# Weighted sums over index heads: one product of 128 stationary columns per sequence, or four products of 32 stationary columns for two sequences

## The chip, the cores and the metric

The kernel runs on one core of a Trainium2 chip. The metric is the device time of one execution in microseconds (us). One program computes both layers; there is one launch.

## The reference

One inference step of a two-layer hybrid decoder trunk for a prompt of 1024 tokens and 8 sample sequences of 8 new tokens each, with 8192 cached positions per sample sequence. Three parallel head groups (mLSTM, indexer-selected sparse attention, RWKV-7) read one combined input projection. The part that the change touches is the indexer of the sample sequences:

```
def index_scores(iq, iw, ik, mask):
    s = jnp.einsum('bthd,bsd->bths', iq.astype(jnp.float32), ik.astype(jnp.float32))
    s = jax.nn.relu(s * IDX_DIM ** -0.5)
    score = jnp.einsum('bths,bth->bts', s, iw.astype(jnp.float32) * IDX_HEADS ** -0.5)
    return jnp.where(mask[None], score, -jnp.inf)
```

For every sequence b, new token t and cached position s the dot products of 8 index heads h with the cached index key are taken, cut at zero, and summed over the heads with the token's weights. The 256 highest scores of a token then select the cached rows that are attended to. All arithmetic is float32.

## The kernel before, in words

The front stage (stage_front, line 149) runs once per layer, before all other stages, and stages are separated by barriers of all engines. On TensorE it walks through 72 units (UNITS, line 171), one for each pair of a 512-column slice of the input projection and a tile of 128 tokens: `unit(u)` makes 8 products of 128x128 by 128x512 (line 396), the evictions from PSUM are ScalarE's (line 518), and the first 36 units are rotated by VectorE, transposed by TensorE (line 422) and copied out (line 611).

The indexer's work is spread between these products. A piece J is one sequence's block of 1024 cached keys. There are 64 such pieces, PIECES = 8 blocks for each of DB = 8 sequences, the sequence running fastest (m = J // 8 is the block, b = J % 8 the sequence), and 8 pieces more for the new keys (J from 64 on). Units 10 to 27 take RATE = 4 pieces each, and each piece stands behind a quarter of the unit's projection. For a piece:

- GpSimd gathers two halves of the keys into one of RING = 6 buffers by two indirect DMAs (line 378), six pieces ahead, each as soon as the transposes of the piece that held the buffer are done (semaphore kt_p).
- `turn` (line 431) transposes them, 8 transposes of 128x128 onto 64 columns, into pt[0] and pt[1]; VectorE copies one half (line 640), ScalarE the other (line 534) into kt[J % 2]. The transposes of one piece wait for both copies of the piece before.
- `score` (line 440) is one product of the keys with the queries laid out as a block diagonal, into pi[J % 2], 512 columns: row f*64 + h*8 + t for half f, head h and token t. It waits for the relu of the piece two before.
- `relu` on ScalarE (line 525) goes from pi[J % 2] to rl[J % 2], and waits until the weighted sum of piece J-2 is done.
- `weigh` (line 452) multiplies rl by a stationary 128x128 slice of the table pk ("pick"), which holds the head weights of sequence b in the columns f*64 + b*8 + t and zeros elsewhere. The 8 sequences of a block accumulate in one bank, acc, so that row f*64 + b*8 + t of acc is the score of that token for half f. The piece's work on TensorE is issued as score(J), turn(J+2), weigh(J-1).
- `place` on VectorE (line 646) copies acc into the table of scores s after every 8 pieces; the next block's first weigh waits for it.

For the new keys the products are smaller: score is 64x64 (line 442), weigh 64x128 by 64 columns (line 454).

From unit 29 on VectorE finds the 256th highest score in 32 rounds of counting over the whole table (line 658). TensorE adds up each count after the projection of a unit (line 478). After the last projection two small products (lines 491 and 492) close the ranking, VectorE writes the last tables (lines 707 to 710), and the stage's last DMAs store them.

Every float32 product appears in the trace as two pairs of a stationary load (PEld) and a pass over the moving columns (PE); a transpose appears as one pair.

Of the kernel before, what the change touches and what calls it, by code (L numbers as in the profile page):

```python
# [12 lines left out]
ACT = mybir.ActivationFunctionType  # L13
# [3 lines left out]
P = 128  # L17
# [4 lines left out]
DB = 8  # L22
DT = 8
NS = DB * DT
# [3 lines left out]
HD = 64  # L28
# [120 lines left out]
def stage_front(nc, l, io, sc, const):  # L149
# [23 lines left out]
    NJ = TURNED + DB  # L173
# [3 lines left out]
    BITS = 31  # L177
    N = HALF + NS

    def pieces(u):  # L180
        return range(RATE * (u - START), RATE * (u - START + 1)) if START <= u < ENDED else ()

    with Stage(nc) as st:
# [25 lines left out]
        iwc = st.sb("iw_cols", [P, 2, DB])  # L209
        pk = st.sb("pick", [P, DB * (P + DT)])  # L210
        kt = [st.sb(f"ikT{b}", [P, 4, P]) for b in range(2)]
        rl = [st.sb(f"relu{b}", [P, 512]) for b in range(2)]

        bit = st.sb("bit", [P, BITS], I32)
        bit_f = st.sb("bit_value", [P, BITS])
# [12 lines left out]
        acc = st.ps("p_score", [P, 512])  # L228
        pt = [st.ps(f"pt{i}", [P, 4, P]) for i in range(2)]
        pi = [st.ps(f"pi{i}", [P, 512]) for i in range(2)]  # L230
# [16 lines left out]
        with nc.Block() as block:  # L247
# [119 lines left out]
            @block.gpsimd  # L367
            def _(pool):
                pool.memset(iq[:, :, :, :, :], 0.0).then_inc(zeroed, 1)  # L369
                pool.memset(pk[:, :], 0.0).then_inc(zeroed, 1)  # L370
                pool.wait_ge(idx_r, 1)
                for J in range(TURNED):
                    m, b = J // DB, J % DB
                    if J >= RING:

                        pool.wait_ge(kt_p, J - RING + 1)
                    for f in range(2):
                        pool.indirect_dma_start(ring[J % RING][:, f, :, :].rearrange("p o d -> p (o d)"), None, table,  # L378
                                                bass.IndirectOffsetOnAxis(ap=idx[:, m, 2 * b + f:2 * b + f + 1], axis=0)).then_inc(got[J % RING], 16)

            @block.tensor
            def _(pe):
                def turn_in(o):
                    pe.wait_ge(normed, o + 1)
                    if o:
                        pe.wait_ge(nT_ready, 2 * o)
                    for k in range(KT):
                        ins = pe.transpose(pt[k // 4][:, k % 4, :], xn[o % 2][:, k * P:(k + 1) * P], ident[:, :])
                        if k % 4 == 3:
                            ins.then_inc(xT_psum, 1)  # L390

                def slice_of(u, k0, k1):
                    c, t = UNITS[u]
                    w, cw = (ws, SMALL) if c == IK else (wb[(c - 1) % 2], 512)
                    for k in range(k0, k1):
                        ins = pe.matmul(pp[u % 2][:, 0:cw], nT[:, k, t * P:(t + 1) * P], w[:, k, 0:cw], start=(k == 0), stop=(k == KT - 1))  # L396
                    if k1 == KT:
                        ins.then_inc(chunk_done, 1)

                def unit(u):  # L400
                    c, t = UNITS[u]
                    if c == IK:
                        pe.wait_ge(ws_loaded, 32)
                        pe.wait_ge(nT_ready, 2 * ORDER.index(t) + 2)
                    else:

                        pe.wait_ge(w_loaded[(c - 1) % 2], 16 * ((c - 1) // 2 + 1))
                    if u >= 2:
                        pe.wait_ge(chunk_out, u - 1)
                    n = len(pieces(u)) or 1  # L410
                    for i in range(n):
                        slice_of(u, KT * i // n, KT * (i + 1) // n)
                        if pieces(u):
                            piece(pieces(u)[i])

                def turn_out(u):
                    c, _ = UNITS[u]
                    pe.wait_ge(rotated, u + 1)
                    pe.wait_ge(turned_out, u)
                    v = qo[u % 2] if c in (IK, Q) else pr[u % PR]  # L420
                    for j in range(TURNS[c]):
                        ins = pe.transpose(ptx[:, j, :], v[:, j * P:(j + 1) * P], ident[:, :])
                    ins.then_inc(turned, 1)

                def turn(J):
                    pe.wait_ge(got[J % RING], 32 * (J // RING + 1))
                    if J:
                        pe.wait_ge(kt_r, 2 * J)
                    for f in range(2):
                        for o in range(RUN):  # L430
                            ins = pe.transpose(pt[f][0:HD, o, :], ring[J % RING][:, f, o, :], ident[:, :])  # L431
                    ins.then_inc(kt_p, 1)

                def score(J):
                    b = J % DB
                    if J >= 2:
                        pe.wait_ge(i_r, J - 1)
                    if J < TURNED:
                        pe.wait_ge(kt_r, 2 * J + 2)
                        ins = pe.matmul(pi[J % 2][:, :], iq[:, b, :, :, :].rearrange("p a h t -> p (a h t)"), kt[J % 2][:, :, :], start=True, stop=True)  # L440
                    else:
                        ins = pe.matmul(pi[J % 2][0:HD, 0:NS], iq[0:HD, b, 0, :, :].rearrange("p h t -> p (h t)"), ikn[:, :], start=True, stop=True)
                    ins.then_inc(i_p, 1)

                def weigh(J):
                    m, b = J // DB, J % DB
                    pe.wait_ge(i_r, J + 1)
                    if b == 0 and m:
                        pe.wait_ge(placed, m)
                    w = pk[:, b * P:(b + 1) * P]  # L450
                    if m < PIECES:
                        ins = pe.matmul(acc[:, :], w, rl[J % 2][:, :], start=(b == 0), stop=(b == DB - 1))
                    else:
                        ins = pe.matmul(acc[:, 0:NS], w[0:HD, :], rl[J % 2][0:HD, 0:NS], start=(b == 0), stop=(b == DB - 1))
                    ins.then_inc(w_p, 1)

                def piece(J):
                    score(J)
                    if J + 2 < TURNED:
                        turn(J + 2)  # L460
                    if J:
                        weigh(J - 1)

                def step(u):
                    if 2 <= u < TILES:
                        turn_in(u)
                    if u == START:
                        pe.wait_ge(nT_ready, 2 * TILES)
                        turn(0)
                        turn(1)  # L470
                        pe.wait_ge(iq_r, 1)
                    unit(u)
                    if u == ENDED:
                        weigh(NJ - 1)
                    k = u - COUNT0 - 1
                    if 0 <= k <= BITS:
                        pe.wait_ge(counted, k + 1)
                        pe.matmul(ptot[:, k:k + 1], pair, cnt[:, k:k + 1], start=True, stop=True).then_inc(total, 1)
                    elif k == BITS + 2:
                        pe.wait_ge(fin_c, 1)  # L480
                        pe.matmul(pfin[:, 0:2], pair, fin[:, :], start=True, stop=True)
                        pe.matmul(pfin[:, 2:3], below, fin[:, 1:2], start=True, stop=True).then_inc(fin_p, 1)
                    if 2 <= u < NTURN + 2:
                        turn_out(u - 2)

                turn_in(0)
                turn_in(1)
                for u in range(NU):
                    step(u)
                pe.wait_ge(ranked, 1)  # L490
                pe.matmul(pfin[:, 3:4], below, s[:, HALF - 1:HALF], start=True, stop=True)
                pe.matmul(pfin[:, 4:5], pair, s[:, HALF - 1:HALF], start=True, stop=True).then_inc(rank_p, 1)

            @block.scalar
            def _(act):
# [23 lines left out]

                def relu(J):  # L520
                    act.wait_ge(i_p, J + 1)
                    if J >= 2:
                        act.wait_ge(w_p, J - 1)
                    if J < TURNED:
                        ins = act.activation(rl[J % 2][:, :], pi[J % 2][:, :], ACT.Relu, scale=HD ** -0.5)
                    else:
                        ins = act.activation(rl[J % 2][0:HD, 0:NS], pi[J % 2][0:HD, 0:NS], ACT.Relu, scale=HD ** -0.5)
                    ins.then_inc(i_r, 1)

                def copy_kt(J):  # L530
# [5 lines left out]
                def piece(J):  # L536
                    relu(J)
                    if J + 2 < TURNED:
                        copy_kt(J + 2)
# [3010 lines left out]
```

## Time and profile before

| | |
|---|---|
| median of 3 runs | 6780.59 us |
| the three runs | 6777.11, 6780.59, 6792.77 us |
| the profiled execution, span from its first to its last instruction | 6785.8 us |
| mean granted TensorE clock | 0.868 |
| front stage, layer 0 (from the start to the last tables at 718.0 us) | about a tenth of the span |
| TensorE busy | 5678.2 us, 84% of the span |
| VectorE, ScalarE, GpSimd busy | 2916.9, 1480.2, 741.8 us |

The profile gives no time for the profiled execution besides its span. In the profile, PE is TensorE's passes and PEld its stationary loads (they overlap the passes), DVE is VectorE, ACT is ScalarE, POOL is GpSimd, SP is SyncE. L452 is line 452 of the kernel. The form 128*32 would be a stationary operand of 128 rows and 32 columns, and 128x512 a moving operand of 128 rows and 512 columns. The granted clock is a share of 2.4 GHz. The end of a pass is modelled, so that the durations of neighbouring passes overlap; the distance between starts tells how long TensorE was taken up. The second layer's front stage repeats the first's.

### The profile page before, as it was taken

The page shows a single profiled execution, that of the slowest core. Times are in us where ns is not written, and L with a number is a line of the kernel's source. Part 1 is how long each engine was busy: PE and PEld are TensorE (multiplying, and loading weights), DVE is VectorE, ACT ScalarE, POOL GpSimd, SP SyncE. Part 2 cuts the span into 40 slices and gives each one's busy share as a digit, 9 for nine tenths or more (in the row PEclk, how much of TensorE's full clock was granted, in tenths as well). Part 3 has the DMA queues.
Part 4 walks back from the last instruction along what each step waited for, and adds up shares of the span by engine and source line. Part 5 has one row for each costly group of instructions (what it writes and reads, how often), then busy time and mean ns, then how long its engine had stood idle before and what let it go on. Part 6 is the DMA issues. An engine that isn't in the chain of part 4 may idle for free. (4 is left out here: it accounts for less than half of the span.)

```text
span 6785.8 us, 62816 instructions
## 1 busy us (share of the span) xinstructions
PE 5678.2 (84%) x22554; PEld 3493.1 (51%) x22554; DVE 2916.9 (43%) x6698; ACT 1480.2 (22%) x2844; POOL 741.8 (11%) x776
## 2 busy tenths in 40 slices
PE   6999686465789899999989996863757879999997
PEld 4544464344567456654455444642545664666543
DVE  2257564367644233330032566533775442334200
ACT  2210122046243111100033102221553331110000
POOL 2400175000000000000033003740000000000000
PEclk9999688575789999999989996975757889999998
DMA  4222233120000231121132313322000013211122
GB/s 148 87 93 81 72 109 95 27 67 15 11 19 5 111 131 50 57 69 59 50 117 82 107 68 89 110 71 68 26 14 19 11 61 120 76 57 50 58 74 93
DMA packets 358055, 462.83 MB, mean 68 GB/s; under 512 B 70258, under 2 KB 261172, under 8 KB 357332
## 3 DMA queue, kind: packets, MB, share of 16 engines
q1 hardware_dynamic: 320932, 358.82, 16.4%
q0 software_dynamic: 36864, 100.71, 4.8%
q8 instruction: 144, 2.36, 0.1%
q14 instruction: 115, 0.94, 0.0%
HBM read 347.87 MB, written 121.69 MB: 69 GB/s over the span
## 5 line engine op out<-in xcount | busy, mean ns | idle before, releaser
L396 PE MATMUL pp<-w_in,nT 128*128 128x512 f32 x2016 | 909.3, 597 | 0.0
L3309 PE MATMUL pm<-w_down,hT 128*128 128x512 f32 x1584 | 685.5, 596 | 24.3 <-DMA hT<-scratch_hT 24.3
L3236 PE MATMUL pg<-nT,wgu 128*128 128x364 f32 (+1 forms) x2112 | 670.1, 471 | 16.5 <-DMA wgu<-in_w_up 16.5
L3236 PE MATMUL pu<-nT,wgu 128*128 128x364 f32 (+1 forms) x2112 | 665.1, 468 | 0.0
L396 PEld LDWEIGHTS pp<-w_in,nT 128*128 128x128 f32 x2016 | 375.6, 191 | 428.0 <-issue 427.3
L3236 PEld LDWEIGHTS pg<-nT,wgu 128*128 128x128 f32 x2112 | 403.7, 191 | 261.1 <-issue 21.1
L3236 PEld LDWEIGHTS pu<-nT,wgu 128*128 128x128 f32 x2112 | 401.4, 190 | 242.2
L3309 PEld LDWEIGHTS pm<-w_down,hT 128*128 128x128 f32 x1584 | 302.9, 191 | 406.4 <-issue 406.4
L2478 POOL DMA_INDIRECT k_sel<-in_cache_k,kv_idx x256 | 247.4, 966 | 985.2 <-DVE kv_idx L2622 860.1
L3261 DVE TENSOR_SCALAR sig<-exp_neg 128x364 f32<-128x364 f32 x132 | 46.1, 349 | 680.6 <-ACT exp_neg L3247 680.6
L3262 DVE RECIPROCAL exp_neg<-sig 128x364 f32<-128x364 f32 x132 | 319.4, 2419 | 4.5
L3327 DVE TENSOR_TENSOR x_tile<-pm,x_tile 128x512 f32<-128x512 f32 x36 | 24.9, 691 | 685.1 <-PE pm L3309 685.1
L378 POOL DMA_INDIRECT ik<-in_cache_idx_k,idx x256 | 245.0, 957 | 390.2 <-PE pt L431 338.2
L658 DVE TENSOR_SCALAR_CACHE_REDUCE area<-s,cand 128x4160 f32<-128x4160 f32 x62 | 281.8, 4546 | 2.2
L3247 ACT ACTIVATE exp_neg<-pg 128x364 f32<-128x364 f32 x132 | 62.3, 472 | 953.1 <-PE pg L3236 952.8
L2478 POOL DMA_INDIRECT v_sel<-in_cache_v,kv_idx x256 | 245.4, 959 | 99.0 <-issue 72.8
L3101 PE MATMUL pm<-w_out,yT 128*128 128x512 f32 x576 | 252.9, 597 | 0.0
L369 POOL MEMSET iq_diag<- 128x1024 f32 x2 | 1.9, 951 | 2284.6 <-issue 2257.1
L640 DVE COPY ikT<-pt 64x512 f32<-64x512 f32 x128 | 87.3, 682 | 372.8 <-PE pt L431 372.8
L518 ACT ACTIVATE proj<-pp 128x512 f32<-128x512 f32 (+1 forms) x144 | 79.5, 552 | 697.2 <-PE pp L396 690.1
L2162 ACT ACTIVATE area<-score,cand 128x768 f32<-128x768 f32 (+2 forms) x192 | 198.0, 1032 | 116.2 <-DVE cand L2311 113.1
L2101 PE MATMUL bank<-kT,qT 64*128 64x512 f32 (+3 forms) x384 | 179.1, 579 | 26.1 <-DVE mx L2281 26.0
(667 smaller groups left out, 8449.5 us busy)
## 6 DMA issues: line engine op xcount, KB each, us to landing
w_in<-in_w_in SPq DMA_DIRECT2D x14, 2048.0 KB, 9.8
scratch_hT<-hT SPq DMA_DIRECT2D x44, 576.0 KB, 2.8
hT<-scratch_hT SPq DMA_DIRECT2D x18, 1408.0 KB, 7.2
wgu<-in_w_gate SPq DMA_DIRECT2D x44, 512.0 KB, 3.9
wgu<-in_w_up SPq DMA_DIRECT2D x44, 512.0 KB, 5.2
w_down<-in_w_down SPq DMA_DIRECT2D x22, 1024.0 KB
x_all<-scratch_x SPq DMA_DIRECT2D x27, 512.0 KB, 15.6
a_tile<-scratch_pa SPq DMA_DIRECT2D x18, 516.0 KB, 4.9
```

The source lines that it names most:

```text
L378: pool.indirect_dma_start(ring[J % RING][:, f, :, :].rearrange("p o d -> p (o d)"), None, table, bass.IndirectOffsetOnAxis(ap=idx[:, m, 2 ...
L396: ins = pe.matmul(pp[u % 2][:, 0:cw], nT[:, k, t * P:(t + 1) * P], w[:, k, 0:cw], start=(k == 0), stop=(k == KT - 1))
L518: act.activation(pr[u % PR][:, 0:cw], pp[u % 2][:, 0:cw], ACT.Copy).then_inc(chunk_out, 1)
L640: dve.tensor_copy(kt[J % 2][0:HD, :, :], pt[0][0:HD, :, :]).then_inc(kt_r, 1)
L658: dve.tensor_scalar(hit, s[:, :], value, 0.0, ALU.is_ge, ALU.add, accum_out=cnt[:, k:k + 1]).then_inc(counted, 1)
L2101: pe.matmul(bk[n % 2][:, 0:cw], qT[e, kv // 2 * 2 + g, i * P:(i + 1) * P], kT[e, kv // 2, c0:c0 + cw], start=True, stop=True).then_inc(s_p, 1)
L2162: act.activation(rank[:, off[i]:off[i] + width(i)], acc[:, off[i]:off[i] + width(i)], ACT.Sign, bias=cand[:, n:n + 1].bitcast(F32), scale= ...
L2478: pool.indirect_dma_start(tiles[n % RING][:, f, :], None, table, bass.IndirectOffsetOnAxis(ap=k_idx[:, n, f:f + 1], axis=0)).then_inc(got[ ...
L3101: ins = pe.matmul(pm[t % 2][n][:, :], yT[t % 2][:, k, :], w[:, k, n * 512:(n + 1) * 512], start=(k == 0), stop=(k == KT - 1))
L3236: ins = pe.matmul(bank[:, 0:cw], wb[b][:, which, k, :], nT[:, k, c0:c0 + cw], start=(k == 0), stop=(k == KT - 1))
L3262: chain(dve.reciprocal(e[m % 2][:, 0:cw], sg[m % 2][:, 0:cw]))
L3309: ins = pe.matmul(pm[b][n][:, :], h[b][:, k, :], w[:, k, n * 512:(n + 1) * 512], start=(k == 0), stop=(k == FT - 1))
```

## The change

Two sequences' pieces are summed together. Pieces are taken in another order of sequences (`seq_of`: 0, 4, 1, 5, 2, 6, 3, 7), so that an even piece J has a sequence of the first four and piece J+1 one of the last four. The scores of sequences 0 to 3 stand in rows 0 to 31 (half 0) and 64 to 95 (half 1) of acc, those of sequences 4 to 7 in rows 32 to 63 and 96 to 127. Where before each piece had one product of 128 stationary columns, each pair of pieces now has four products of 32 stationary columns, one for each half and sequence; they write to the partitions 0, 32, 64 and 96 onward of the bank acc, in that order. For the new keys the two products stay as they were and are issued together. There are four relu buffers instead of two, and the weigh of a pair is issued in the even piece after it.

```diff
+    def seq_of(J):
+        return J % 2 * (DB // 2) + J % DB // 2
...
-        rl = [st.sb(f"relu{b}", [P, 512]) for b in range(2)]
+        rl = [st.sb(f"relu{b}", [P, 512]) for b in range(4)]
...
                 for J in range(TURNED):
-                    m, b = J // DB, J % DB
+                    m, b = J // DB, seq_of(J)
...
                 def score(J):
-                    b = J % DB
+                    b = seq_of(J)
...
                 def weigh(J):
-                    m, b = J // DB, J % DB
-                    pe.wait_ge(i_r, J + 1)
-                    if b == 0 and m:
+                    m = J // DB
+                    pe.wait_ge(i_r, J + 2)
+                    if J % DB == 0 and m:
                         pe.wait_ge(placed, m)
-                    w = pk[:, b * P:(b + 1) * P]
                     if m < PIECES:
-                        ins = pe.matmul(acc[:, :], w, rl[J % 2][:, :], start=(b == 0), stop=(b == DB - 1))
+                        for f in range(2):
+                            for k in range(2):
+                                b = seq_of(J + k)
+                                r = f * NS + b // (DB // 2) * 32
+                                ins = pe.matmul(acc[r:r + 32, :], pk[:, b * P + r:b * P + r + 32], rl[(J + k) % 4][:, :], start=(J % DB == 0), stop=(J % DB == DB - 2))
                     else:
-                        ins = pe.matmul(acc[:, 0:NS], w[0:HD, :], rl[J % 2][0:HD, 0:NS], start=(b == 0), stop=(b == DB - 1))
-                    ins.then_inc(w_p, 1)
+                        for k in range(2):
+                            b = seq_of(J + k)
+                            ins = pe.matmul(acc[:, 0:NS], pk[0:HD, b * P:(b + 1) * P], rl[(J + k) % 4][0:HD, 0:NS], start=(J % DB + k == 0), stop=(J % DB + k == DB - 1))
+                    ins.then_inc(w_p, 2)

                 def piece(J):
                     score(J)
                     if J + 2 < TURNED:
                         turn(J + 2)
-                    if J:
-                        weigh(J - 1)
+                    if J and J % 2 == 0:
+                        weigh(J - 2)
...
                     if u == ENDED:
-                        weigh(NJ - 1)
+                        weigh(NJ - 2)
...
                 def relu(J):
                     act.wait_ge(i_p, J + 1)
-                    if J >= 2:
-                        act.wait_ge(w_p, J - 1)
+                    if J >= 4:
+                        act.wait_ge(w_p, J // 2 * 2 - 2)
                     if J < TURNED:
-                        ins = act.activation(rl[J % 2][:, :], pi[J % 2][:, :], ACT.Relu, scale=HD ** -0.5)
+                        ins = act.activation(rl[J % 4][:, :], pi[J % 2][:, :], ACT.Relu, scale=HD ** -0.5)
```

## Rows read from the trace of the kernel before

**Rows 1.** Stretches: busy us by engine, then PEclk, DMA share, GB/s.
```profile
120.00:375.00 255.00, 255.00 (x981) 139.30 (x980) 72.20 (x177) 77.10 (x130) 98.30 (x104) 1.00 0.23 77
410.00:640.00 230.00, 230.00 (x600) 106.81 (x599) 166.42 (x216) 19.28 (x33) 0.00 (x0) 1.00 0.29 103
3488.00:3743.00 255.00, 255.00 (x980) 139.27 (x979) 72.20 (x177) 77.10 (x130) 98.32 (x104) 1.00 0.23 77
```
**Rows 2.** Waits, 100 to 715 us: waiter, releaser, us in total, times, longest.
```profile
DVE ikT L640 <- PE pt L431: 187.1, 63, 3.6
ACT relu L525 <- PE pi L440: 144.3, 64, 3.3
POOL ik L378 <- PE pt L431: 122.9, 57, 2.6
```
**Rows 3.** TensorE in order of time: start, us, line, names, stationary, moving, passes.
```profile
207.62 1.02 PE L440 MATMUL pi<-ikT,iq_diag 128*128 128x512 f32 x2
208.48 1.04 PE L431 MATMUL pt<-c_ident,ik 128*64 128x128 f32 x8
209.35 1.02 PE L452 MATMUL p_score<-relu,pick 128*128 128x512 f32 x2
210.21 1.88 PE L396 MATMUL pp<-w_in,nT 128*128 128x512 f32 x4
211.93 1.02 PE L440 MATMUL pi<-ikT,iq_diag 128*128 128x512 f32 x2
```
**Rows 4.** Order of time: VectorE's first count; end of the stage, TensorE and VectorE.
```profile
418.41 4.55 DVE L658 TENSOR_SCALAR_CACHE_REDUCE area<-s,zero 128x4160 f32<-128x4160 f32 x1
...
714.70 0.28 PE L491 MATMUL p_score<-s,c_masks 128*128 128x1 f32 x2
...
715.23 0.15 DVE L707 COPY c_new_bias<-p_score 64x1 f32<-64x1 f32 x1 [27.33 <-PE p_score L492]
```
**Rows 5.** Line 452, both layers: duration ns min/median/max, first and last start.
```profile
L452 PE MATMUL p_score<-relu,pick x256: 592/593/697, 108.3 to 3751.3; 128*128 128x512 f32 x128
```
**Rows 6.** TensorE in order of time, heads by turns on the two row halves.
```profile
1462.60 2.00 PE L2091 MATMUL bank<-ikT,qT 64*128 64x512 f32 x8
1464.53 0.44 PE L1857 MATMUL bank<-sa,M_T 128*128 128x64 f32 x2
```
**Rows 7.** TensorE in order of time, changes between 64 and 128 rows.
```profile
381.34 1.45 PE L396 MATMUL pp<-w_in,nT 128*128 128x512 f32 x3
382.72 0.33 PE L442 MATMUL pi<-ik_new,iq_diag 64*64 64x64 f32 x2
382.97 1.12 PE L452 MATMUL p_score<-relu,pick 128*128 128x512 f32 x2
383.94 1.88 PE L396 MATMUL pp<-w_in,nT 128*128 128x512 f32 x4
...
386.36 1.98 PE L396 MATMUL pp<-w_in,nT 128*128 128x512 f32 x4
388.28 0.33 PE L442 MATMUL pi<-ik_new,iq_diag 64*64 64x64 f32 x2
```
**Rows 8.** TensorE in order of time, products on half the columns.
```profile
952.21 0.68 PE L2853 MATMUL bank<-v,kw 128*64 128x65 f32 x8
952.82 0.55 PE L2504 MATMUL bank<-c_ident,k_sel 128*128 128x128 f32 x3
```
**Rows 9.** A piece's work on ScalarE and VectorE; the gathers and their landing.
```profile
208.68 0.60 ACT L525 ACTIVATE relu<-pi 128x512 f32<-128x512 f32 x1 [3.29 <-PE pi L440]
...
209.55 0.68 DVE L640 COPY ikT<-pt 64x512 f32<-64x512 f32 x1 [1.83 <-PE pt L431]
210.41 1.04 DVE L646 COPY s<-p_score 128x512 f32<-128x512 f32 x1 [0.18 <-PE p_score L452]
...
L378 POOL DMA_INDIRECT ik<-in_cache_idx_k,idx x256: 940/945/1985, 33.7 to 3715.5; - x128
...
DMA to landing us min/median/max: 2.6/2.7/6.7
```

More of the change, by code:

```diff
@@ L521, in relu @@
                     act.wait_ge(i_p, J + 1)
-                    if J >= 2:
-                        act.wait_ge(w_p, J - 1)
+                    if J >= 4:
+                        act.wait_ge(w_p, J // 2 * 2 - 2)
                     if J < TURNED:
-                        ins = act.activation(rl[J % 2][:, :], pi[J % 2][:, :], ACT.Relu, scale=HD ** -0.5)
+                        ins = act.activation(rl[J % 4][:, :], pi[J % 2][:, :], ACT.Relu, scale=HD ** -0.5)
                     else:
-                        ins = act.activation(rl[J % 2][0:HD, 0:NS], pi[J % 2][0:HD, 0:NS], ACT.Relu, scale=HD ** -0.5)
+                        ins = act.activation(rl[J % 4][0:HD, 0:NS], pi[J % 2][0:HD, 0:NS], ACT.Relu, scale=HD ** -0.5)
                     ins.then_inc(i_r, 1)
```

## The prediction

> **What bounds the kernel now.** I read four views in this order. First the stretches of the front stage, because the change touches nothing else. TensorE is busy in 255.00 of 255.00 us between 120 and 375 us in layer 0, in 255.00 of 255.00 at the same place of layer 1, and in 230.00 of 230.00 from 410 to 640 us, all at a granted clock of 1.00, 2.4 GHz; VectorE is at 72 of 255 us, ScalarE at 77, GpSimd at 98 [rows 1]. Then the waits: ScalarE, VectorE and GpSimd wait for TensorE's scores, transposes and projections in total for 144, 187 and 123 us, and no row has TensorE waiting for data [rows 2]. So the stage is a single queue of TensorE work, and whatever is taken out of this queue moves everything behind it, if no other engine comes last. Third, TensorE's queue in order of time. One piece is 8 transposes, one weighted sum, a quarter of a projection and one score. The sum starts at 209.35 and its successor at 210.21: 0.86 us for two passes of 512 columns, 0.43 each. A whole piece from 207.62 to 211.93 is 4.31 us [rows 3]. Fourth, the end of the stage: the projections run until 714.70 and VectorE has by then waited 27.33 us for the last small product [rows 4], so the end too is set by TensorE.
>
> **What the change removes.** Line 452 has 256 passes, that is 128 products in two layers [rows 5]. A pair of them takes 2 x 0.86 = 1.72 us [rows 3]. There are 32 pairs a layer, 64 in all, 110 us of TensorE's queue.
>
> **What it adds.** In place of a pair stands a group of four products on 32 stationary columns each, every one still of 512 moving columns and two passes, so 8 passes. One after the other they would take 8 x 0.43 = 3.44 us, twice what was there. All hangs on whether the four column quarters work at the same time. The trace has no case of two column quarters next to each other; it has row halves. Line 2091 puts heads by turns on rows 0 to 63 and 64 to 127. At 1462.60 eight of its passes of 512 columns begin and the next product begins at 1464.53: 1.93 us where 8 x 0.43 is 3.44 [rows 6]. So two products of fp32, each of two passes, run side by side, and the second product's first pass does not wait for the first one's second. I take the same for columns.
>
> Fixed costs come from the same trace, since a product of another array shape does not follow smoothly. (a) The switch: three passes of line 396 begin at 381.34 and should be followed at 382.63; the 64*64 product begins at 382.72, 0.09 us late [rows 7]. (b) After a switch the stationary load is not hidden: the sum that starts at 382.97 takes 0.97 us instead of 0.86, so 0.11 us for 128 columns [rows 7]. (c) Both again at the other side: four passes from 386.36 to 388.28 are 1.92 us, not 1.72 [rows 7]. (d) A column shape costs the same: eight passes of 65 columns on half the columns begin at 952.21 and the full shape follows at 952.82, 0.61 us; the passes are 8 x 0.055 = 0.44, leaving 0.17, which is one switch and one load of 64 columns and a little [rows 8]. Transposes onto 64 columns pay no switch (208.48 follows two passes from 207.62 at once, [rows 3]), so the group pays its own, in and out.
>
> The group: switch in 0.09; load of 32 columns 0.03 (a quarter of 0.11); stream of one product 0.86; switch out 0.09; load of the 128 columns of what comes next 0.11. That is 1.18 without any offset between the four. The offset is not shown for columns. Below, it is the 0.01 us that the row halves had (1.93 less 4 x 0.43, 0.09 and 0.11, [rows 6, 7]). Above, the loads of all eight passes go one by one through one door, so that the fourth product's first load is the seventh: 6 x 0.027 = 0.16 us. I take one load per product, 3 x 0.027 = 0.08, between the two, since first passes evidently need not wait for second ones. Group 1.26 us; gain 1.72 - 1.26 = 0.46 us; 64 x 0.46 = 29.6 us. By the lower offset 64 x 0.53 = 34 us, by the upper 64 x 0.38 = 24 us.
>
> A page of the Trainium skill, "TensorE: Matmul & The Clock Gate", section "Measured speedup vs the span model", gives 2.38 times for three products of 32 stationary columns and 512 moving ones and an offset of some 4 ns each. By that rule the offset would be 0.012 and the gain 34 us. The row halves agree with it more or less (0.01 us); for columns no run here shows it, and the rule's products are not said to be of two passes.
>
> **Small edits.** The last 8 pieces of a layer (new keys) put two sums of 64 columns together. The four lone turns from a 64*64 score to a 64*128 sum disappear, about 0.1 us each [rows 7]; 0.4 us a layer, about 1 us in all. The reordering of sequences (seq_of) changes which column of a table is read, on GpSimd and TensorE, and no size; two more relu buffers are room in SBUF. Both cost nothing. A group has 8 passes where the pair had 4, and their issue is in the group's price; they bring no waits of their own.
>
> **Waits.** The new wait for relu stands at the even piece J and asks for relu(J-1). On TensorE between the score of J-1 and this sum lie a transposition of 0.87 us, a quarter of a projection of 1.72, a score of 0.86 and another 0.87: 4.3 us, against 0.60 us of relu [rows 3, 9]. Relu itself waits for the group before the last, one piece longer ago than its data; with four buffers nothing is queued up behind it. Odd pieces lose their sum, which was cover for the copies of the transposed keys: from one piece's transposes to the next 1.72 + 0.86 = 2.58 us of TensorE remain. The copies end at 210.23, 0.88 us after the transposes have made way at 209.35 [rows 3, 9], so the cover stays, with 1.7 us over; if it failed the copy would cost 0.7 us a pair at most. VectorE's placing of a block (1.04 us) is done by the next piece, and the next group comes two pieces later instead of one. GpSimd's gathers cost 2 x 0.945 us a piece with landing in 2.7 us [rows 9] and TensorE's piece is 8.16 / 2 = 4.08 on the mean afterwards; six slots are about 24 us ahead. The clock was 1.00 before, and gaps of 0.2 us do not empty the engine.
>
> **Sum.** 29.6 + 1 = 30.6 us off a profiled span of 6785.8 gives 6755.2. The page gives the span and no more of that execution; the median of the three runs is 5.2 us below it, 6780.6. Forecast 6750 us.
>
> **Rivals.**
> 1. *Three together, the fourth alone, or two and two.* The four products stream two different relu tiles from the same 128 partitions at once, which row halves never did (each reads its own 64 partitions): this is what speaks for it. The place is the group itself; the price is a second stream, 1.26 + 0.86 = 2.12 us, 0.40 more than the pair; 64 x 0.40 = 25 us slower: 6805 with the small edits. It decides as soon as a group needs more than the 0.46 us that it has to spare beyond one stream and its fixed costs. In the Trainium skill, "TensorE: Matmul & The Clock Gate", section "Step-by-step: what each phase is for", the bus for the high columns is said to be not supported, which would make just the fourth wait; no run here shows it.
> 2. *Start in strict order with two passes each.* Pass two of a product holds up the next product: five streams, 5 x 0.43 + 0.40 = 2.55, 0.83 more, 53 us slower: 6833. Rows 6 speak against it.
> 3. *No concurrency at all*: 3.44 + 0.40 = 3.84, 2.12 more, 136 us slower: 6915. Nothing for it but the absence of a column case.
> 4. *Partly concurrent or with offsets of 0.1 us and over per product*: group 1.5 to 1.7, gain 1 to 13 us: 6773.
> 5. *The gain does not come to the end* (copies or stage end): 6779. Rows 2 and 4 speak against it.
>
> **How the numbers follow.** Forecast 0.73, rival 1 0.08, rival 2 0.05, rival 3 0.04, rival 4 0.07, rival 5 0.03. The likeliest case's own range is 6738 to 6764: 24 to 34 us of gain and 6 us for the scatter that the three runs show. The range reaches through rival 4 and the nearer half of what lies beyond, to 6790. Within 0.2% (13.6 us, about what a measurement of this kernel tells from no change) lie rival 5 and most of rival 4: 0.09. Faster 0.74, slower 0.17.
>
> **What would show it.** In the front stage two pieces should last 8.62 - 0.46 = 8.16 us; the group of eight passes should have starts within 0.2 us for the first four and its successor about 1.1 us after the first start. TensorE should stay without idle, the first count on VectorE (418.41 us in layer 0, [rows 4]) should come 15 us sooner, and everything after it at unchanged distances. The forecast is wrong if the starts of the group's passes are 0.43 us apart, or if ScalarE's or VectorE's copies appear as releasers of TensorE.

## The result and the profile after

The changed kernel takes 6738.64 us (median of 4 runs, 6737.09 to 6740.28) against 6778.85 us before (4 runs, 6776.51 to 6792.77): ratio 0.9943, interval 0.9929 to 0.9957, that is 29 to 48 us less. Two later comparisons of the same two kernels gave 0.9956 (0.9943 to 0.9969) and 0.9947 (0.9928 to 0.9967). Forecast was 6750; the two profiled spans are 6785.8 and 6738.3 us.

First the stretches, as in [rows 1] (busy us by engine, granted clock, DMA share, GB/s). TensorE is still busy without a break at clock 1.00 in the stretch with sums and in the one with counts.

```profile
120.00:360.00 240.00, 240.00 (x1095) 121.33 (x1093) 72.12 (x184) 76.84 (x130) 96.10 (x101) 1.00 0.25 81
386.00:616.00 230.00, 230.00 (x599) 106.65 (x598) 166.40 (x215) 19.11 (x32) 0.00 (x0) 1.00 0.29 103
```

TensorE in order of time, two pieces of the changed kernel, the counterpart of [rows 3]:

```profile
194.45 1.02 PE L444 MATMUL pi<-ikT,iq_diag 128*128 128x512 f32 x2
195.31 1.04 PE L435 MATMUL pt<-c_ident,ik 128*64 128x128 f32 x8
196.28 1.06 PE L459 MATMUL p_score<-relu,pick 128*32 128x512 f32 x8
197.27 1.98 PE L400 MATMUL pp<-w_in,nT 128*128 128x512 f32 x4
199.09 1.02 PE L444 MATMUL pi<-ikT,iq_diag 128*128 128x512 f32 x2
199.95 1.04 PE L435 MATMUL pt<-c_ident,ik 128*64 128x128 f32 x8
200.82 1.88 PE L400 MATMUL pp<-w_in,nT 128*128 128x512 f32 x4
202.54 1.02 PE L444 MATMUL pi<-ikT,iq_diag 128*128 128x512 f32 x2
```

Eight passes of 512 columns begin at 196.28 and their successor at 197.27: 0.99 us, where one stream of two passes is 0.86 and eight in a row would be 3.44. That all four products start together can be read off directly. The passes of this group that run before 196.30, and then all of its passes:

```profile
L459 PE MATMUL p_score<-relu,pick x4: 617/617/617, 196.3 to 196.3; 128*32 128x512 f32 x4
L459 PE MATMUL p_score<-relu,pick x8: 592/604/617, 196.3 to 196.8; 128*32 128x512 f32 x8
```

So four passes, the first of each product, start between 196.28 and 196.30, and the other four follow, the last at 196.8. The price of the change of shape is there on both sides. Transposes lead to a product of the full shape in 0.87 us ([rows 3], 208.48 to 209.35) and to the group in 0.97; the four passes behind the group take 1.82 us and not 1.72. So the group costs 0.10 + 0.99 + 0.10 = 1.19 us, and two pieces take 202.54 - 194.45 = 8.09 us where they took 8.62.

The score products of layer 0, before and after (durations ns min/median/max, then the start of the first and of the last pass):

```profile
L440 PE MATMUL pi<-ikT,iq_diag x128: 592/592/593, 103.1 to 379.2; 128*128 128x512 f32 x128
```

```profile
L444 PE MATMUL pi<-ikT,iq_diag x128: 592/592/593, 96.6 to 356.3; 128*128 128x512 f32 x128
```

This stretch, from a layer's first score to its last, holds 31 of a layer's 32 groups. It went from 276.1 to 259.7 us, 16.4 us or 0.53 a group. The first count of VectorE now starts at 394.29 us, where it was 418.41 [rows 4], and the last products of the stage at 690.57 and not 714.70: 24.1 us earlier both times, so all that happens between is unchanged. Of the 24.1 us 6.5 were gone before the first score (103.1 against 96.6), which the sums can't have brought, as none has run by then; 17.6 are left. The experiments start from there.

```profile
394.29 4.54 DVE L667 TENSOR_SCALAR_CACHE_REDUCE area<-s,zero 128x4160 f32<-128x4160 f32 x1
```

```profile
690.57 0.28 PE L500 MATMUL p_score<-s,c_masks 128*128 128x1 f32 x2
```

### The profile page after: what moved, and what is told of

Its sections match the earlier page's. It is cut to its first block and busy times, and to the rows that moved or that the text cites. A ratio compares the mean times of both kernels' runs of the same rounds, so it can differ in the third digit from the quotient of the medians.

```text
span 6738.3 us, 63246 instructions
## 1 busy us (share of the span) xinstructions
PE 5627.2 (84%) x22732; PEld 3448.6 (51%) x22810; DVE 2914.1 (43%) x6698; ACT 1481.2 (22%) x2844; POOL 743.5 (11%) x776
## 5 line engine op out<-in xcount | busy, mean ns | idle before, releaser
L3318 PE MATMUL pm<-w_down,hT 128*128 128x512 f32 x1584 | 686.1, 596 | 24.1 <-DMA hT<-scratch_hT 24.1
L3245 PE MATMUL pg<-nT,wgu 128*128 128x364 f32 (+1 forms) x2112 | 671.1, 471 | 16.4 <-DMA wgu<-in_w_up 16.4
```

What stands on the lines that cost most here:

```text
L3245: ins = pe.matmul(bank[:, 0:cw], wb[b][:, which, k, :], nT[:, k, c0:c0 + cw], start=(k == 0), stop=(k == KT - 1))
L3318: ins = pe.matmul(pm[b][n][:, :], h[b][:, k, :], w[:, k, n * 512:(n + 1) * 512], start=(k == 0), stop=(k == FT - 1))
```

## The experiments

The theory (A): the four column quarters work at the same time, a group costs 1.19 us instead of 1.72, and the rest of the 47.5 us between the two profiles is scatter between executions. Rivals: (B) start-up and later stages gain as well; (C) the issue in pairs and the longer relu ring bring part of it; (D) four streams at once are slower than two.

**1. The kernel before, once more** (no edit).

> The kernel before, unchanged, profiled a second time. The two profiles at hand differ by 47.5 us in span, of which the stretches with weighted sums hold 17.6 us in each layer; 6 us are gone before the first weighted sum and the rest comes and goes in later stages that the change doesn't touch. Theory A (those are scatter between executions): ratio 1.000, span of this profile 6774 to 6780, and its first transposed keys come 5 to 6 us earlier than in the first profile. Theory B (the change does something to start-up): span again about 6786 and the start as late as before.

Measured: ratio 1.0007 (0.9995 to 1.0018), span 6778.2 us. All score products of both layers, in the first profile and in this one:

```profile
L440 PE MATMUL pi<-ikT,iq_diag x256: 592/592/593, 103.1 to 3747.0; 128*128 128x512 f32 x128
```

```profile
L440 PE MATMUL pi<-ikT,iq_diag x256: 592/592/593, 101.9 to 3737.2; 128*128 128x512 f32 x128
```

Within layer 0 the stretch is again 276.1 us (101.9 to 378.0). The last score of layer 1 comes 9.8 us earlier, of which 1.2 us lie before the first score and 8.6 us in the stages between the layers' front stages. So one and the same kernel scatters by 8.6 us there, and the span fell to within what A expected. The place that A had named for it was wrong: the start came 1.2 us earlier and not 5 to 6. All 35 runs of this kernel that were timed for experiments 1 to 4 lie between 6765 and 6806 us.

**2. The changed kernel, once more** (no edit).

> The changed kernel, unchanged, on the same chip as the others. Theory A: the gain is 64 groups x 0.53 us = 34 us plus 1 us at the new keys, ratio 0.9949 (0.994 to 0.996). Theory B (start-up and later stages gain too): 42 us or more, ratio 0.9938 or less.

Measured: 0.9956 (0.9943 to 0.9969), median 6746.51 against 6775.37 us; span 6735.3. First score at 99.0 and last of layer 0 at 358.8: again 259.8 us, but a start 2.4 us later than in the first profile. That is A's size and not B's. What start-up and the other stages showed in the first pair of profiles isn't of the change: in the profiles of the later experiments the first score comes anywhere from 97.7 to 102.8 us, and with the full-shape sums of experiment 3 at 98.0.

**3. Pairs only.** Order of sequences, four buffers and issue in pairs stay; the products are the old ones.

```diff
-                        for f in range(2):
-                            for k in range(2):
-                                b = seq_of(J + k)
-                                r = f * NS + b // (DB // 2) * 32
-                                ins = pe.matmul(acc[r:r + 32, :], pk[:, b * P + r:b * P + r + 32], rl[(J + k) % 4][:, :], ...)
+                        for k in range(2):
+                            b = seq_of(J + k)
+                            ins = pe.matmul(acc[:, :], pk[:, b * P:(b + 1) * P], rl[(J + k) % 4][:, :], ...)
```

> The changed kernel with two products of 128 stationary columns in place of the four of 32; the order of sequences, the four relu buffers and the issue in pairs stay. Theory A (all of the gain is the column quarters working at once): no change against before but the 1 us at the new keys, ratio 0.9998 (0.999 to 1.001). Theory C (issue in pairs and the longer relu ring bring part of it): 5 us or more faster, ratio 0.999 or less.

Measured: 1.0006 (0.9995 to 1.0017). The stretch is 276.1 us, as before (first row); the two sums in a row follow the transposes in 0.87 us and take 1.72:

```profile
L444 PE MATMUL pi<-ikT,iq_diag x128: 592/592/593, 98.0 to 374.1; 128*128 128x512 f32 x128
```

```profile
193.46 1.04 PE L435 MATMUL pt<-c_ident,ik 128*64 128x128 f32 x8
194.33 1.88 PE L457 MATMUL p_score<-relu,pick 128*128 128x512 f32 x4
196.05 1.88 PE L400 MATMUL pp<-w_in,nT 128*128 128x512 f32 x4
```

C falls: apart from the 0.6 us a layer at the new keys (table below) nothing of the gain is the pairing's. This also settles a row of the changed kernel that looks like a wait. Of the group's passes and loads (line 459) it says what ended the idle time before them, in us and times:

```profile
  ACT relu L534: 11.8, 60
```

That would be 0.2 us for nearly every group. But the relu that the group waits for belongs to the piece before and has long been done: for the group at 196.28 it ended at 192.22, and the one that ended just before the group, at 196.11, is not waited for. With the same waits, in the same places, the full-shape sum here follows with no gap. The idle time is the switch, put down to the last semaphore event.

**4. Two of the four products left out.**

```diff
-                        for f in range(2):
+                        for f in range(2 if J == 0 else 1):
...
-                                ins = pe.matmul(..., start=(J % DB == 0), stop=(J % DB == DB - 2))
+                                ins = pe.matmul(..., start=(J % DB == 0), stop=(J % DB == DB - 2 or f == 1))
```

> The changed kernel without the two products for the second half of the keys (column quarters 2 and 3), except in the very first group: it leaves out half of each weighted sum. Theory A (each further quarter costs its offset of about 7 ns and nothing else): 64 x 0.014 = 1 us faster than the changed kernel, ratio to before 0.994 to 0.996. Rival (the quarters share something, so that four streams are slower than two): a stream shorter than 0.86 us is impossible, so it can only show as a group clearly shorter than 0.98 us from first start to successor, or as 5 us or more.

Measured: 0.9964 (0.9952 to 0.9977), just outside the expected 0.994 to 0.996, with an interval that doesn't tell it from the changed kernel's ratios. The trace does: the stretch is 259.4 us (100.8 to 360.2), 0.3 less than with four, and a group goes from its first start to its successor in 0.98 us where four took 0.99:

```profile
191.87 1.05 PE L459 MATMUL p_score<-relu,pick 128*32 128x512 f32 x4
192.85 1.99 PE L400 MATMUL pp<-w_in,nT 128*128 128x512 f32 x4
```

The first of the 31 groups still has all four products, so two more quarters cost 0.3 / 30 = 0.01 us a group. D falls.

**5. All four products on one quarter.**

```diff
-                                ins = pe.matmul(acc[r:r + 32, :], pk[:, b * P + r:b * P + r + 32], ...)
+                                ins = pe.matmul(acc[0:32, :], pk[:, b * P + r:b * P + r + 32], ...)
+                        if J == 0:
+                            pe.matmul(acc[32:64, :], pk[:, 0:32], rl[0][:, :], start=True, stop=True)
+                            ins = pe.matmul(acc[64:128, :], pk[:, 0:64], rl[0][:, :], start=True, stop=True)
```

The start and stop flags of the first product are fitted to the single quarter. The two products added write the other quarters once a layer, in its first group.

> The changed kernel with all four products of a group on the first column quarter; what is summed in the other quarters is left out. Theory A (the gain is concurrency between quarters): a group takes 8 passes one after the other, 3.44 + 0.3 us, 2.0 us more than the pair of before, 64 x 2.0 = 130 us slower than before, about 6910. Rival (small stationary operands are themselves cheaper): clearly under 3.4 us a group.

Measured: 6893.28 us, ratio 1.0171 (1.015 to 1.0191), 102 to 130 us slower; about 6910 was expected. The stretch is 340.0 us, 63.9 more than before; the first group, with its two added products, holds 1.0 of that (106.46 to 111.02, 4.56 us), which leaves 62.9 / 31 = 2.03 a group. Eight passes now take 3.55 us:

```profile
L444 PE MATMUL pi<-ikT,iq_diag x128: 592/592/593, 97.7 to 437.7; 128*128 128x512 f32 x128
```

```profile
192.78 1.04 PE L435 MATMUL pt<-c_ident,ik 128*64 128x128 f32 x8
193.74 3.62 PE L459 MATMUL p_score<-relu,pick 128*32 128x512 f32 x8
197.29 1.98 PE L400 MATMUL pp<-w_in,nT 128*128 128x512 f32 x4
```

That is the changed kernel without concurrency: from the second group on the same number of passes, the same stationary size, the same waits. A pass on 32 columns takes as long as one on 128, 0.43 us, and the whole gain is that the four products run side by side. From the second score to the first count the trace has 65.2 us a layer more than before (table below), 130 in both, which is the upper end of the interval; the times outside the stretch scatter, and two runs don't settle them.

**6. Two halves of 64 columns.**

```diff
-                        for f in range(2):
-                            for k in range(2):
-                                b = seq_of(J + k)
-                                r = f * NS + b // (DB // 2) * 32
-                                ins = pe.matmul(acc[r:r + 32, :], pk[:, b * P + r:b * P + r + 32], ...)
+                        for k in range(2):
+                            b = seq_of(J + k)
+                            r = 64 * k
+                            ins = pe.matmul(acc[r:r + 64, :], pk[:, b * P + r:b * P + r + 64], ...)
```

> The changed kernel with two products of 64 stationary columns per pair on the two column halves (half of the sums is left out, each sequence's wrong half included). Theory A: stream 0.86, switches 0.19, load of 64 columns 0.05 in place of 0.03, load out 0.11: 1.21 us a group, the gain of the changed kernel less 1 us, ratio 0.9950. Rival (four small streams cost more than two larger ones): faster than the changed kernel by 3 us or more.

Measured: 0.9952 (0.9938 to 0.9967). The stretch is 260.2 us (102.8 to 363.0), 0.5 more than with quarters, or 0.02 a group: half as many passes, a little slower. From the group's first start to its successor's are 1.01 us and not 0.99. The larger first load accounts for it: first passes last up to 644 ns on line 458 here and 617 in the quarters, 592 where the load is hidden:

```profile
194.10 1.08 PE L458 MATMUL p_score<-relu,pick 128*64 128x512 f32 x4
195.11 1.98 PE L400 MATMUL pp<-w_in,nT 128*128 128x512 f32 x4
```

**7 and 8. Longer groups.** If switches and uncovered loads are paid once a group, fewer groups should pay. The sums of 4 pieces, then of 8, are issued together; the relu ring has 5 buffers, then 9 (four of them the tiles xn, idle by then). The sums of the new keys are issued 4 and 8 at a time too. Cut to its core, for 8:

```diff
-        rl = [st.sb(f"relu{b}", [P, 512]) for b in range(4)]
+        rl = [st.sb(f"relu{b}", [P, 512]) for b in range(5)] + [xn[n][:, c:c + 512] for n in range(2) for c in (0, 512)]
...
-                    pe.wait_ge(i_r, J + 2)
+                    pe.wait_ge(i_r, J + 8)
...
+                        for j in range(J, J + 8, 2):
...
-                    if J and J % 2 == 0:
-                        weigh(J - 2)
+                    if J and J % 8 == 0:
+                        weigh(J - 8)
...
-                    if J >= 4:
-                        act.wait_ge(w_p, J // 2 * 2 - 2)
+                    if J >= 9:
+                        act.wait_ge(w_p, ((J - 9) // 8 + 1) * 8)
```

> The changed kernel with weighted sums of four pieces issued as one group (8 products, two on each quarter), five relu buffers. Theory A (the fixed cost of a group, 0.34 us of switches and uncovered loads, is paid per group, whatever its length): half the groups, 32 x 0.33 = 10.7 us faster than the changed kernel, ratio to before about 0.9934. Rival (ScalarE's relu falls behind, or products on the same quarter don't follow without a gap): the same as the changed kernel or slower.

> As before it, with the whole block of eight pieces as one group (16 products, four on each quarter), nine relu buffers. Theory A: 16 groups instead of 64, 48 x 0.33 = 16 us faster than the changed kernel, ratio to before about 0.9925. Rival (a queue of 32 passes and loads in a row is held up by issue, or the burst of 3.4 us makes ScalarE, VectorE and the gathers late): less than the gain of groups of four.

Measured: 0.9948 (0.9933 to 0.9964) for 4, 0.9936 (0.9922 to 0.9949) for 8; 0.9934 and 0.9925 were expected. Whole runs tell neither from the changed kernel (0.9943 to 0.9956); the stretch does. The scores of layer 0 for 4 and for 8, and a group of 4 pieces, 16 passes in 1.85 us:

```profile
L444 PE MATMUL pi<-ikT,iq_diag x128: 592/592/593, 99.5 to 353.1; 128*128 128x512 f32 x128
```

```profile
L444 PE MATMUL pi<-ikT,iq_diag x128: 592/592/593, 100.5 to 349.7; 128*128 128x512 f32 x128
```

```profile
196.34 1.92 PE L460 MATMUL p_score<-relu,pick 128*32 128x512 f32 x16
198.19 1.98 PE L400 MATMUL pp<-w_in,nT 128*128 128x512 f32 x4
```

16 passes in 1.85 are four passes in a row on each quarter, 4 x 0.43, and the same extra of 0.13 that 8 passes had over their 2 x 0.43. From the group's first start to the successor's and with 0.20 around it, a group of 4 pieces costs 2.05 us where two groups of 2 cost 2.38: 0.33 saved by each group that goes. A group of 8 pieces has no gap either, 32 passes in 230.42 - 226.85 = 3.57 us or 8 x 0.43 + 0.13 (four of the nine relu buffers bear the name xn):

```profile
226.85 1.48 PE L460 MATMUL p_score<-xn,pick 128*32 128x512 f32 x9
...
230.42 1.98 PE L400 MATMUL pp<-w_in,nT 128*128 128x512 f32 x4
```

The rivals (ScalarE late, gaps between products on one quarter, 32 passes held up by issue) fall. How much of a layer is saved, the last group included, shows in the time from a layer's second score, the last one before any sum, to VectorE's first count, here for all versions (the same in both layers within 0.01 us, and in every further profile of the same kernel). The expectation of experiment 9 calls this second score the third; the numbers are the same:

| kernel | second score to first count, us a layer |
|---|---|
| before | 311.88 |
| pairs only | 311.29 |
| the changed kernel | 294.27 |
| two of four | 293.86 |
| two halves | 294.70 |
| groups of 4 | 288.67 |
| groups of 8 | 285.87 |
| one quarter | 377.06 |

Groups of 4 save 5.6 us a layer against the changed kernel and groups of 8 save 8.4; 5.3 and 8 were expected.

**9 and 10. Changed kernel and groups of 8 side by side** (no new edit).

> The changed kernel a third time, beside the groups of eight on the same chip, because whole executions of every version scatter by 10 us and more while the stretch from the third score to the first count repeats within 0.01 us (294.27 us a layer here). Theory A: the stretch again 294.27 us in both layers, ratio to before 0.9948, that is 35 us faster.

> The groups of eight again, beside the changed kernel. The stretch is 8.40 us a layer shorter than the changed kernel's (285.87 us). Theory A (what the stretch gives arrives at the end): 16.8 us faster than the changed kernel, ratio to before 0.9924. Rival (part of it is lost in the later stages): 8 us or less between the two.

Measured: 0.9947 (0.9928 to 0.9967) and 0.993 (0.9911 to 0.9949). On this chip every kernel took longer, the one before 6947.73 us, but not in the stretch, which is 259.8 and 249.2 us as elsewhere. Of the 147 us between the profiled runs of experiments 2 and 9, 74 lie between the first count of layer 0 and the first score of layer 1; what slows those stages stays open.

```profile
L444 PE MATMUL pi<-ikT,iq_diag x128: 592/592/593, 99.4 to 359.2; 128*128 128x512 f32 x128
```

```profile
L444 PE MATMUL pi<-ikT,iq_diag x128: 592/592/593, 101.8 to 351.0; 128*128 128x512 f32 x128
```

By the ratios groups of 8 are 12 us faster than the changed kernel here (0.9947 against 0.9930) and 14 us by experiments 2 and 8 (0.9956 against 0.9936). Either difference is within what the two intervals leave open, and the medians here (6 and 5 runs) are only 3 us apart, 6907.89 and 6904.86 us, which fits the rival (8 us or less); the ratios are not simply those of the medians. So the gain of 16.8 us in the front stages is shown, and how much of it arrives at the end is not.

## Why the prediction was right

**What bounds.** Right: TensorE's queue stayed full and all after the sums moved up by what they saved.

**Concurrency of column quarters.** Right, and taken from row halves alone. The first passes of the four products start within 0.02 us, as the sign named in the prediction asks (0.2 us). Two more quarters add 0.01 us (experiment 4), and experiment 5 shows what it would be without: 2.03 us a group more than before, where rival 3 had 2.12.

**Fixed costs.** Right. On the way in, 0.09 us for the switch and 0.03 for the load were forecast, and 0.10 (0.97 less 0.87) and 0.03 (passes of 617 ns where others have 592) were found. On the way out, 0.09 and 0.11 were forecast; found were 0.08 (0.99 less 0.86, 0.03 and the offset of 0.02 of the next paragraph) and 0.10 (1.82 less 1.72). That this is a price per group is shown by experiments 7 and 8.

**The offset between products.** The one term that was mis-sized. I took 0.08 us a group for the loads to pass one by one, and it is 0.02, or 7 ns for each product after the first (two quarters more cost 0.01). A group is 1.19 us and not 1.26, the gain 0.53 and not 0.46, which is what my lower end for the offset gave. The rule of the Trainium skill, "TensorE: Matmul & The Clock Gate", section "Measured speedup vs the span model", was nearer than my choice: some 4 ns a product, 0.012 us for three, where this trace has 0.020 with float32 products of two passes. The gain in the sums is then 64 x 0.53 = 34 us, and with the new keys 35.2 (17.6 in each layer up to the first count).

**Small edits.** Right: pairing alone is worth 0.6 us a layer; 0.4 was forecast, rounded up to 1 us in all.

**Waits.** Right: nothing became late. I had written that copies of ScalarE or VectorE as releasers of TensorE would prove the forecast wrong. ScalarE does appear as one, with its relu, and not because TensorE waited for it (experiment 3). So this sign was badly chosen.

**The sum.** 30.6 us were forecast (64 x 0.46 is 29.4 and not 29.6, which changes nothing). The stages give 35.2, and the three comparisons of whole runs 30 to 39 (0.9956, 0.9947, 0.9943). 6738.64 is 11 us below the forecast of 6750 and less than 1 us inside the likeliest case's range: nearly 5 us of that are the offset, 2 the lower median before (6778.85 and not 6780.6), and the other 5 scatter, since the medians of this comparison differ by 40.2 us where the stages give 35.2. That the number still fell within that range was luck in this last part; the mechanism was not.

**Rivals.** 1 (the fourth product alone, or two and two) falls by the starts of the four first passes and by experiment 4, and with it the reading that the Trainium skill's sentence on the high columns, in "TensorE: Matmul & The Clock Gate", section "Step-by-step: what each phase is for", would make the fourth wait; the trace doesn't agree with that, as the fourth starts 0.02 us after the first. 2 and 3 fall by the same rows, 4 by the group's 1.19 us. 5 falls by the first count and by the three comparisons, none of whose intervals reaches 1.

## What to carry to other kernels

When a stationary operand is mostly zeros, look for an order of the work in which its filled columns fall into different quarters: four products of 32 columns took 1.19 us where two of 128 took 1.72, since a pass of 512 moving columns took 0.43 us with 32 or 128 stationary columns and passes on different quarters ran side by side. The change of shape costs about 0.33 us a group, in and out, so put as many products as buffers allow between two changes (0.33 us less for each group saved). And where whole executions scatter by 10 us and more, time the change in its own stretch, which here repeated to within 0.1 us in seven profiles of three kernels; whether a gain of that size also shows at the end is a second question, which the groups of 8 left open.

## What the runs showed of the hardware

- Products on four column quarters, float32 with two passes each, run side by side: 8 passes in 0.99 us, 16 in 1.85, against 3.55 for 8 on a single quarter. Each further product starts 7 ns after the one before. I had seen this for row halves only [rows 6].
- The two relu tiles that the quarters stream lie in the same 128 partitions; four streams at once cost 0.01 us more than two.
- Idle time at a change of array shape is put down to whatever semaphore came last, here to ScalarE 60 times (11.8 us), with no wait behind it.
- On one of the chips the same kernels took 160 to 170 us longer, with no difference in the TensorE-bound stretch.
